# VectorE takes the minima of a pair of attention heads two pairs ahead, and the first attention's pairs lose their dropped products

## What is computed

```python
for hd in range(16):                       # 256 queries in two tiles of 128 rows
    logits = q[hd] @ k[hd].T * 64 ** -0.5  # 128 keys for tile 0, 256 for tile 1 (causal)
    logits = logits + bias[hd]             # the mask of the selection, or the relative bias
    p = softmax(logits)                    # over the keys
    o[:, hd] = p @ v[hd]
h = h + o.reshape(256, 1024) @ w_o
```

## Time and profile before

| | |
|---|---|
| median of 3 runs | 996.75 us (994.36 to 997.92) |
| the profiled execution | 988.9 us, of it 987.2 us from the first to the last instruction |
| TensorE busy | 944.6 us (96%), granted clock 0.998 of 2.4 GHz |
| VectorE, ScalarE, GpSimd busy | 606.8, 464.2, 138.3 us |
| 64 to 110 us, TensorE waits for others | 3.4 us: 2.3 for minima (6 times), 1.1 for `out_lo` (once) |
| 700 to 777 us, TensorE waits | 0.4 us, once, for minima |

### The profile page before, as it was taken

One profiled execution on the slowest core, in us unless ns is written; L12 is line 12 of the kernel. 1 busy time (PEld: TensorE's weight loads), 2 busy tenths in 40 slices (PEclk: granted clock), 3 DMA queues, 4 the chain that ended last, 5 costly groups with the idle time before them and its releaser, 6 DMA issues.

```text
span 987.2 us, 11869 instructions
## 1 busy us (share of the span) xinstructions
PE 944.6 (96%) x4717; PEld 779.5 (79%) x4717; DVE 606.8 (61%) x960; ACT 464.2 (47%) x616; POOL 138.3 (14%) x115
## 2 busy tenths in 40 slices
PE   6779999999999998999999999999999999999996
PEld 5657788888887787998788888877787778888885
DVE  4674676464648756978755464585323567767775
ACT  4565344252433453254443433345566465556562
POOL 3163200000001810001100000001174110101010
PEclk9999999999999999999999999999999999999999
DMA  8891356556547653224765655467433355555531
GB/s 281 189 165 34 120 191 199 184 185 199 173 154 228 231 175 108 88 83 128 247 200 173 199 182 187 154 212 256 152 132 123 128 169 190 175 180 187 186 129 42
DMA packets 103510, 165.89 MB, mean 168 GB/s; under 512 B 3931, under 2 KB 72570, under 8 KB 103456
## 3 DMA queue, kind: packets, MB, share of 16 engines
q1 hardware_dynamic: 99968, 152.61, 47.0%
q0 software_dynamic: 3488, 12.53, 5.7%
HBM read 160.93 MB, written 4.19 MB: 167 GB/s over the span
## 4 chain that ended last, share of the span: by engine, by line
PE 84%; DVE 9%; ACT 3%; DMA 2%; issue 1%; POOL 1%; DVEq 0%; POOLq 0%; ACTq 0%
PE PG L1758 12%; PE PG L1760 12%; PE PG L1759 12%; PE PA L1758 12%; PE PA L1760 11%; PE PA L1759 11%; PE PA L2161 2%; DVE wlo L586 1%; PE PG L1890 1%; ACT whi L577 1%; PE TB L2292 1%; PE TB L1907 1%; PE TB L2002 1%; DVE xlo L1070 1%; DVE stats L1132 1%
## 5 line engine op out<-in xcount | busy, mean ns | idle before, releaser
L586 DVE TENSOR_TENSOR wlo<-raw,whi 128x2048 fp32r<-128x2048 f32 (+1 forms) x129 | 300.5, 2345 | 80.5 <-ACT whi L577 80.4
L577 ACT ACTIVATE whi<-raw 128x2048 fp32r<-128x2048 f32 (+1 forms) x142 | 268.5, 1907 | 52.6 <-PE PA L1760 19.5
L1758 PE MATMUL PG<-whi,xlo 128*128 128x512 f32 x560 | 223.2, 399 | 4.0 <-DVE wlo L1288 2.9
L1760 PE MATMUL PG<-whi,xhi 128*128 128x512 f32 x560 | 219.1, 391 | 0.0
L1759 PE MATMUL PG<-wlo,xhi 128*128 128x512 f32 x560 | 218.7, 391 | 0.0
L1758 PE MATMUL PA<-whi,xlo 128*128 128x512 f32 (+1 forms) x344 | 137.5, 400 | 10.1 <-DVE xlo L1070 5.2
L1760 PE MATMUL PA<-whi,xhi 128*128 128x512 f32 (+1 forms) x344 | 132.7, 386 | 0.0
L1759 PE MATMUL PA<-wlo,xhi 128*128 128x512 f32 (+1 forms) x344 | 132.4, 385 | 0.0
L1758 PEld LDWEIGHTS PG<-whi,xlo 128*128 128x128 f32 x560 | 105.8, 189 | 26.0 <-DVE wlo L1288 3.3
L1760 PEld LDWEIGHTS PG<-whi,xhi 128*128 128x128 f32 x560 | 105.5, 188 | 22.6
L1759 PEld LDWEIGHTS PG<-wlo,xhi 128*128 128x128 f32 x560 | 105.8, 189 | 20.6
(11 more groups left out here) (264 smaller groups left out, 1084.2 us busy)
## 6 DMA issues: line engine op xcount, KB each, us to landing
raw<-in_ffn_w_gate SPq DMA_DIRECT2D x44, 512.0 KB, 4.0
raw<-in_ffn_w_up SPq DMA_DIRECT2D x44, 512.0 KB, 5.0
raw<-in_ffn_w_down SPq DMA_DIRECT2D x22, 1024.0 KB, 4.8
raw<-in_w_up SPq DMA_DIRECT2D x44, 512.0 KB, 4.8
raw<-in_hgrn_w_in SPq DMA_DIRECT2D x16, 1024.0 KB, 5.3
raw<-in_w_qkv SPq DMA_DIRECT2D x12, 1024.0 KB, 5.2
raw<-in_w_down SPq DMA_DIRECT2D x11, 1024.0 KB, 4.9
raw<-in_att_w_o SPq DMA_DIRECT2D x4, 1024.0 KB, 5.7
```

Source lines behind the costliest of these rows:

```text
L577: nc.scalar.activation(whi[:, g, 0:n_], raw[:, s, 0:n_], ACT.Copy).then_inc(S("w_hi"), 1)
L586: nc.vector.tensor_tensor(wlo[:, s, 0:n_], raw[:, s, 0:n_], whi[:, g, 0:n_].bitcast(F32), ALU.subtract).then_inc(S("w_lo"), 1)
L1758: mm(dst, xl[:, k, rows], whi[:, g, cols], start=first, stop=False)
L1760: return mm(dst, xh[:, k, rows], whi[:, g, cols], start=False, stop=last_)
```

## The change

It moves VectorE's minima within both attentions, and takes away dropped matmuls in the first.

- Prologue: `minima(2)` and `minima(3)` are taken before the loop, behind heads 0 and 1.
- Pair p takes the minima of pair p+2: head 2p+4 ahead of `output(2p)`, head 2p+5 between `output(2p)` and `output(2p+1)`. In the second attention pair 2 is in `late` on VectorE as it is on TensorE, and takes both behind its outputs.
- A head from 4 on writes over the slot of head hd - 4 in `pr`, so it waits until that head has been transposed.
- In the first attention the `keep_warm(3)` and `keep_warm(2)` of pairs 0, 1 and 2 go, 15 matmuls. The five of the prologue stay. Nothing of the result is left out by that.

```diff
-            def attention(tag, bias, first_minima):
+            def attention(tag, bias, first_minima, late=()):
                 def minima(hd):
                     vec.wait_ge(S("logit" + tag), hd // 2 + 1)
+                    if hd >= 4:
+                        turned(turned_p[tag][hd - 4])
...
                 minima(0)
                 minima(1)
                 first_minima()
+                minima(2)
+                minima(3)
                 for p in range(PAIRS):
-                    if p + 1 < PAIRS:
-                        minima(2 * p + 2)
                     if p and p - 1 in OUT_AFTER[:3]:
                         out_lo(tag, OUT_AFTER.index(p - 1))
                     turn_out(2 * p)
                     ready = reciprocals(p)
-                    if p + 1 < PAIRS:
-                        minima(2 * p + 3)
+                    ahead = p + 2 < PAIRS
+                    if ahead and p not in late:
+                        minima(2 * p + 4)
                     vec.wait_ge(S("vec_chain"), ready)
                     output(2 * p)
+                    if ahead and p not in late:
+                        minima(2 * p + 5)
                     output(2 * p + 1)
+                    if p in late:
+                        minima(2 * p + 4)
+                        minima(2 * p + 5)
...
-                      lambda: lo(U_M + 8))
+                      lambda: lo(U_M + 8), (2,))
...
             def turned_first(p):
-                if p < 3:
-                    keep_warm(3)
...
             def outputs_made(p):
-                if p < 3:
-                    keep_warm(2)
```

## The result

| | kernel before | changed kernel |
|---|---|---|
| first measurement, median | 995.78 us (994.36 to 997.92, 4 runs) | 988.93 us (988.11 to 989.76, 4 runs) |
| ratio | 1 | 0.9929, 95% interval 0.9906 to 0.9953 |
| profiled execution, span | 987.2 us | 988.0 us |
| its mean granted clock | 0.998 | 0.989 |

The kernel is faster by 6.9 us, 0.7%. The two profiles say the opposite of the medians: the changed kernel's profiled execution is 0.8 us longer. That contradiction is the subject of this part.

The account below looks back on a forecast made before the run. TensorE, with 84% of the chain, was held up by logits waiting for VectorE's minima. 2.2 + 0.55 + 0.66 + 0.52 + 0.50 = 4.4 us off 996.75 gave 992.3 us, range 990.0 to 996.0.

Parts of the forecast that it names:

- The ring of minima and logits: First attention, pairs 0 to 2: logits wait for VectorE's minima behind the outputs; taking minima a pair earlier gains 2.2 us.
- ScalarE is the next: Pairs 0 to 2: ScalarE's queue, 4.05 us in pairs 0 and 1, becomes the bound, 0.8 us behind TensorE's own work.
- The dropped products: First attention: worth little in pairs 0 and 1; two after pair 2, ahead of turn_out_rows, are on the path, 0.55 us.
- Logits(5), logits(7), the second attention: Waits between a turn and its logits shrink to 0.42 us: gains of 0.66, 0.52 and, in second-attention pair 5, 0.50 us.
- The later output(2p+1): Pairs 0 to 2: output(2p+1) starts 0.25 to 0.35 us later behind minima; covered by ScalarE's lateness, otherwise 1.05 us.
- the rival's mechanism: Rival, chance 0.20: the wait only moves from logits to TB's banks, as outputs stand behind minima; gain 3.3, 993.4 us.
- The step that failed: Whole kernel: adds to the profiled execution a gap of 7.9 us to the median, taken as untouched by the change.
- The clock as a rival: First attention, pairs 1 to 3: without dropped products TensorE runs at 1.2 GHz, about +3.5 us, 1000.3 us; chance 0.07.
- two windows at 1.00: 40 to 45 and 50 to 55 us: TensorE busy 2.30 and 2.64 of 5 us, in short pieces, clock granted 1.00.
- The rule of the Trainium skill quoted in the prediction: TensorE: small idle pieces between groups of matmuls can make the clock swing between two levels; speaks against removing dropped products.

Follow-up runs that it names:

- units later: changed filled with ScalarE's two weight units split after pairs 3 and 4, not 0 and 1, and minima(2p+5) behind output(2p+1): 987.69 us, ratio 0.9909.
- changed filled: The changed kernel with 38 dropped products put into four waits of TensorE outside the attentions: 985.7 us, ratio 0.9906.
- turn 7 filled: The kernel before with only 4 dropped products ahead of turn(7), in the first attention's wait of 1.09 us: 993.26 us, ratio 0.9985.

## Why the prediction was right about the attentions and wrong about the time

- **The ring of minima and logits** was the bound of pairs 0 to 2, and leaves it. Forecast for pv(5) 2.2 us, by the trace 2.45 (13.37 to 10.92). ScalarE is the next, as said: its two units stand without idle time between, and taking them out of these pairs (with the banks' 0.20 us) gives 0.5 us more. But it leads by less than forecast. The period became 3.42, not 3.0, and with both causes taken away it is still 3.34: the forecast put a turn at about 0.4 us, and two take 1.10. TensorE's own work was put too low, and ScalarE and the banks together decide pv(5) by 0.43 us (10.92 against 10.49 in units later, 76.94 less 66.45), where the forecast had ScalarE ahead by 0.8. The forecast for pv(5) was good because it was read off ScalarE's queue.
- **The dropped products**: worth nothing measurable alone (ratio 1.0011), as they lie in a wait. The trace has logits(5) 17.32 behind logits(1) without them, 0.33 less, for the 0.55 forecast. What the forecast didn't say plainly: with the new order they would be the bound (28.12 against 26.24 us), so the two halves need each other.
- **Logits(5), logits(7), the second attention**: 0.66, 0.52 and 0.50 forecast. By the distances to logits(1), 3.52 us are won at logits(5) (3.41 forecast), 4.03 at logits(7) (3.93), and 0.50 in the second attention. Sum 4.5 us, forecast 4.4.
- **The later output(2p+1)**: two turns wait 0.20 us. From logits(2) to logits(4) that costs 0.17 us (6.85 in changed filled, 6.68 in units later), the rival's mechanism at a sixth of its price of 1.05.
- **The step that failed** is the last one of the sum: "The median shown is 7.9 above that execution, which the change doesn't touch". The change does touch it. The profiled execution was free of falls of the clock, one of the fastest of before in this study; the usual one has several, and one of their places lies in the attention that the change rebuilds. The gap of 0.8% between the profile and the lowest to highest runs (994.36 to 997.92, none near 988.9) was the sign, and I carried it over as a constant. With it understood the size comes out: filling pair 3 alone brings before 1.9 us, and 4.5 + 1.9 = 6.4 us, against 6.9 and 6.7 measured. Counting gives much the same, but roughly: of 66 runs of before that stood beside the kernels above, 44 took 995 us or more. If all of these had the fall in pair 3, it would cost 44/66 x 3.2 = 2.1 us in the mean. One execution with it is known by its trace (996.99 us, not one of the 66), but the profiled 995.2 us of turn 7 filled has none, so some of the 44 may lack it, and some below 995 may have it; at 996.5 us or more there are 25, which gives 1.2 us. How often before falls there no set of traces shows.
- **The clock as a rival** had the wrong sign for the whole change. I asked whether taking products out could make the clock fall, and found two windows at 1.00 an argument against. They were one execution's. Behind the same waits the clock fell to half in other executions, the changed kernel's profiled one among them. The rule of the Trainium skill quoted in the prediction is thus borne out in part, and with the old order: there the clock fell to half behind the waits of 1.09 and 0.53 us in two profiles and stayed at 1.00 behind the same waits in others. The change made TensorE's work denser by taking waits out, though it has fewer products (4.07 us busy of 5 in the window from 80 us in its second profile, against 3.75 in the one of before that falls). Taking the products out without the new order may be another matter, as the two executions near 1000 us say, but no trace shows it. The Trainium skill's page TensorE: Matmul & The Clock Gate also says, under "What's actually happening", that the monitor's cycle runs freely and doesn't start with the kernel. That agrees with what is seen here, an equal program that falls at the same few places in some executions and not in others. What no run shows is which places a given execution will pick.

## What to carry to other kernels

Compare the profiled execution with the timed ones before building a sum on it: where it is faster than all of them, find what the others suffer (here the granted clock, window by window, in a second profile), and ask of each edit whether it touches one of those places. A dropped product that keeps TensorE busy is only worth something in a wait; once the wait goes, it is the bound. In pair 3 taking waits out kept the clock up as filling them did. Taking inputs one stage earlier on an engine that issues in order removed a ring of waits here, at two new ones of 0.20 us.

## What the runs showed of the hardware

- The same binary of the kernel before took from 988.9 to 998.3 us, at mean granted clocks from 0.998 to 0.986; two of 66 took less than 990. In the profiles of both kernels the clock fell to half (0.50 in windows of 1 us) in or behind waits of TensorE, near 41, 56, 376 to 385 and 671 to 680 us, and with the old order in the first attention near 86 us.
- A fall in pair 3 of the first attention cost 3.2 us (33.44 against 30.26 us).
- Dropped products in waits took the falls out of one profile each of before and changed, and brought the median of before from 995.72 to 989.75 us, 0.6%, without shortening any needed work. Three further profiles with the same products had a fall near 62 us (0.68 to 0.78 from 60 to 65).
- The fall in pair 3 had no long stand-still ahead of it: the longest waits were 1.09 and 0.53 us, and TensorE was busy 3.75 us in the 5 before. The same waits in three other profiles of this order were followed by no fall.
